# A decoder step with paged attention and experts: the key steps of the samples moved into the projections, three of four of their products on GpSimd

## What is computed

```python
h = rmsnorm(x);  p = h @ w_in                       # 1024 -> 2560 columns
q, k, v, u = rope(rmsnorm(q)), rope(rmsnorm(k)), v, ua * sigmoid(ub)
# differential attention, 4 heads, 2 components of 64 each, v of 128
a = softmax(q1 k1) - lam * softmax(q2 k2);  o = rmsnorm(a @ v) * (1 - lam_init)
# prompt: causal over 512 tokens.  sample b: over 4096 cached tokens, 32 pages
# of 128 given by page_table, and its own new one
conv = silu(layernorm(causal_depthwise_conv31(u)))
x = x + concat(o, conv) @ w_out
x = x + moe(rmsnorm(x))                             # 32 experts, the best 4 of each token
```

## Time and profile before

| | us |
|---|---|
| median of 3 runs | 1733.65 |
| lowest and highest | 1730.45, 1736.07 |
| the profiled execution | 1735.41 |
| its span in the trace | 1733.7 |
| PE busy | 1474.0 (85%) |
| DVE busy | 782.4 (45%) |
| ACT busy | 356.0 (21%) |
| POOL busy | 96.7 (6%) |

### The profile page before, as it was taken

How to read it: one execution, slowest core, us unless ns; L and a number is a source line. 1 busy time by engine, 2 the same in 40 slices (tenths; PEclk the granted TensorE clock), 3 DMA queues, 4 the chain that set the end, 5 groups by cost and what they waited for, 6 DMA issues and landing times.

```text
span 1733.7 us, 32093 instructions
## 1 busy us (share of the span) xinstructions
PE 1474.0 (85%) x11950; PEld 595.0 (34%) x11951; DVE 782.4 (45%) x1160; ACT 356.0 (21%) x822; POOL 96.7 (6%) x173
## 2 busy tenths in 40 slices
PE   3868887779788978899998998999899999899970
PEld 2433333346433354332332332333233332232320
DVE  2789879997786335221332232132132131131326
ACT  3212212222222111111211211212112122121220
POOL 0000010000000000000100000000000000000000
PEclk8989995679898857999999999999899999999995
DMA  9557888988998785598999999999999999999986
GB/s 327 182 187 258 283 295 272 331 279 292 311 301 270 242 352 207 227 392 339 429 420 403 427 417 396 412 418 411 392 421 412 401 428 411 397 428 399 428 351 253
DMA packets 127292, 598.10 MB, mean 345 GB/s; under 512 B 20503, under 2 KB 20517, under 8 KB 102026
## 3 DMA queue, kind: packets, MB, share of 16 engines
q1 hardware_dynamic: 109088, 560.20, 81.9%
q10 hardware_dynamic: 8634, 20.00, 3.4%
q0 software_dynamic: 9504, 17.06, 2.6%
HBM read 589.36 MB, written 25.87 MB: 355 GB/s over the span
## 4 chain that ended last, share of the span: by engine, by line
PE 40%; DMA 19%; DVE 2%; issue 1%; ACT 0%; DVEq 0%; SPq 0%; ACTq 0%
PE bank L1511 25%; DMA wts<-in_w_gate_up 16%; PE bank L1548 8%; PE bank L1530 4%; DMA wts<-in_w_down 3%; PE bank L1501 1%; PE bank L1618 1%; DVE v_ring L2139 1%; PE bank L1559 1%; PE bank L1599 0%; DVE q_b L2139 0%; DMA h_tok<-h_rows,v_tok 0%; ACT k_T L1155 0%; DVEq L2127 0%; ACT k_T L1138 0%
## 5 line engine op out<-in xcount | busy, mean ns | idle before, releaser
L1511 PE MATMUL bank<-wts,h_T 128*32 128x512 f32 x4032 | 443.9, 597 | 9.7 <-DMA wts<-in_w_gate_up 5.2
L2061 DVE TENSOR_SCALAR q_T<-bank 128x512 f32<-128x512 f32 x32 | 22.1, 692 | 636.9 <-PE bank L1511 636.9
L1511 PEld LDWEIGHTS bank<-wts,h_T 128*32 128x32 f32 x4032 | 129.5, 111 | 308.3 <-issue 296.4
L1548 PE MATMUL bank<-wts,k_T 128*32 128x512 f32 x2048 | 228.3, 597 | 8.0 <-issue 4.9
L1530 PE MATMUL bank<-wts,h_T 128*32 128x512 f32 x992 | 132.6, 675 | 52.2 <-DMA wts<-in_w_gate_up 50.4
L1658 DVE TENSOR_TENSOR wts<-wts,q_b 128x1024 f32<-128x1024 f32 x128 | 158.1, 1235 | 23.1 <-DMA wts<-in_cache_k 17.4
L1661 DVE TENSOR_REDUCE sc<-wts 128x16 f32<-128x1024 f32 x128 | 156.2, 1220 | 4.4
L1145 ACT ACTIVATE h_T<-bank 128x512 f32<-128x512 f32 x66 | 35.9, 595 | 573.5 <-PE bank L1501 573.5
L1548 PEld LDWEIGHTS bank<-wts,k_T 128*32 128x32 f32 x2048 | 64.9, 110 | 149.0 <-issue 139.5
L1223 PE MATMUL bank<-wts,h_T 128*8 128x128 f32 (+1 forms) x480 | 92.7, 465 | 12.3 <-ACT h_T L854 6.4
L1155 ACT ACTIVATE k_T<-bank 32x256 f32<-32x256 f32 x256 | 95.7, 374 | 13.6 <-PE bank L1548 10.2
(11 more groups left out here) (330 smaller groups left out, 1375.8 us busy)
## 6 DMA issues: line engine op xcount, KB each, us to landing
wts<-in_w_gate_up SPq DMA_DIRECT2D x126, 2048.0 KB, 15.8
wts<-in_w_down SPq DMA_DIRECT2D x64, 2048.0 KB, 18.3
wts<-in_cache_k SPq DMA_DIRECT2D x256, 256.0 KB, 3.7
v_ring<-in_cache_v SPq DMA_DIRECT2D x160, 256.0 KB, 3.8
wts<-in_cache_v SPq DMA_DIRECT2D x96, 256.0 KB, 3.9
wts<-in_w_in SPq DMA_DIRECT2D x5, 2048.0 KB, 24.1
wts<-y_rows SPq DMA_DIRECT2D x4, 2048.0 KB, 15.1
wts<-in_w_out ACTq DMA_DIRECT2D x8, 512.0 KB, 6.2
```

The source lines that it names most:

```text
L1511: m = nc.tensor.matmul(PS[part][p0:p0 + 32, :], lhs[:, 32 * b:32 * b + 32], rhs[:, part * F + half * 512:part * F + half * 512 + 512], sta ...
L1548: m = nc.tensor.matmul(PS[4][p0:p0 + 32, :], act_T[0][:, k, a0:a0 + 32], chunk[c][:, k, n * 512:(n + 1) * 512], start=(c == 0 and k == 0), ...
```

## The change

The weights of the schedule change, and 60 of the first 80 key products go to GpSimd. In the projections a key weight of 1 becomes 1.45 (`KEYS`), the value weights stay. In the units the key weights are 0.2 and 0, the value weights 1, 0.9 and 1. In the convolution a stage has 2.5 key and 1.6 value steps in place of 2 and 2, an L stage 1.2 and 1 in place of 1 and 1. For a key step with a number below 80 that is not 3 modulo 4, GpSimd makes the product, as two pieces of 128x512 in place, one for each page, and VectorE waits for them (`kprod_done`) and only sums. For this GpSimd walks the list too; its `tap_w` products and index constants become stages of Q and L. Two sets of semaphores, `xw_loaded` and `y_loaded`, are merged into one, `rows_in`. The core of the diff:

```diff
+        KEYS = 1.45
         for s in range(1, TILES + 1):
             if s > 1:
-                plan(("P", s), 1, both=s > 2)
-            plan(("P", s - 1), 1 if s > 1 else 0, both=s > 2)
-            plan(("P", s), 1 if s > 1 else 3, both=s > 2)
+                plan(("P", s), KEYS, values=1 if s > 2 else 0)
+            plan(("P", s - 1), KEYS if s > 1 else 0, values=1 if s > 2 else 0)
+            plan(("P", s), KEYS if s > 1 else 3, values=1 if s > 2 else 0)
...
-            plan(("P", s), 1)
-            plan(("P", s), 1, 1, 1, both=True)
+            plan(("P", s), KEYS)
+            plan(("P", s), *[KEYS] * 3, values=1)
             if s < TILES:
-                plan(("P", s + 1), 1, both=True)
-            plan(("P", s), 2, values=1)
-            plan(("P", s), 1, 1, both=True)
+                plan(("P", s + 1), KEYS, values=1)
+            plan(("P", s), 2 * KEYS, values=1)
+            plan(("P", s), *[KEYS] * 2, values=1)
...
             if j < UNITS:
-                plan(("Q", j), 1, both=True)
+                plan(("Q", j), 0.2, values=1)
...
             if j < UNITS:
-                plan(("Q", j), 0.4, values=0.7)
+                plan(("Q", j), 0, values=0.9)
...
             if j > 1 and (j - 1) % H == 0:
-                plan(("N", (j - 1) // H), 1, both=True)
-        plan(("V", 0), *[2] * (CT + 1), both=True)
+                plan(("N", (j - 1) // H), 0, values=1)
+        plan(("V", 0), *[2.5] * (CT + 1), values=1.6)
         for n in range(CT + 1):
-            plan(("V", 1), 2, both=True)
-            plan(("L", 0), 1, both=True)
+            plan(("V", 1), 2.5, values=1.6)
+            plan(("L", 0), 1.2, values=1)
...
+        PIECE = 512
+        KEYS_ON_POOL, KEYS_SHARED = (3, 4), 80
+        def on_pool(n):
+            return n < KEYS_SHARED and n % KEYS_ON_POOL[1] < KEYS_ON_POOL[0]
+        def products_on_pool(n):
+            return sum(on_pool(m) for m in range(n + 1)) * GP * (AW // PIECE)
...
+            def key_step(b, g):
+                r, n = g % RING, b * NG + g
+                if not on_pool(n):
+                    return
+                if first_on_pool(b) == g:
+                    pool.wait_ge(qb_in, 32 if b == 0 else 16 * (b + 1))
+                pool.wait_ge(k_full[r], 16 * GP * (4 * b + g // RING + 1))
+                for p in range(GP):
+                    for c0 in range(0, AW, PIECE):
+                        cols = slice(c0, c0 + PIECE)
+                        nc.gpsimd.tensor_tensor(k_ring[:, r, p, cols], k_ring[:, r, p, cols],
+                                                q_b[:, b % 2, cols], ALU.mult).then_inc(kprod_done, 1)
...
-                dve.wait_ge(k_full[r], 16 * GP * (4 * b + g // RING + 1))
-                V.link(mul(k_ring[:, r, :, :], k_ring[:, r, :, :],
-                           q_b[:, b % 2, :].unsqueeze(1).to_broadcast([P, GP, AW])))
+                if on_pool(b * NG + g):
+                    dve.wait_ge(kprod_done, products_on_pool(b * NG + g))
+                else:
+                    dve.wait_ge(k_full[r], 16 * GP * (4 * b + g // RING + 1))
+                    V.link(mul(k_ring[:, r, :, :], k_ring[:, r, :, :],
+                               q_b[:, b % 2, :].unsqueeze(1).to_broadcast([P, GP, AW])))
                 total(sc[:, b % LEAD, GP * g:GP * (g + 1), :],
                       k_ring[:, r, :, :].rearrange("p g (h d) -> p g h d", d=QD)).then_inc(kred_done, 1)
```

More of the change, by code:

```diff
@@ L239, in hybrid_step @@
                 continue
[L240 to L241 removed]
+            plan(("P", s), KEYS)
+            plan(("P", s), *[KEYS] * 3, values=1)
             if s < TILES:
[L243 to L245 removed]
+                plan(("P", s + 1), KEYS, values=1)
+            plan(("P", s), 2 * KEYS, values=1)
+            plan(("P", s), *[KEYS] * 2, values=1)
             if s < TILES:
[L247 to L248 removed]
+                plan(("P", s + 1), KEYS, values=1)
+        plan(("P", TILES), *[KEYS] * 2, values=1)
         plan(("Q", 0), 0)
@@ L341, in hybrid_step @@
         v_full = [sem(f"v_full{n}") for n in range(VRING)]
-        xw_loaded = [sem(f"xw_loaded{n}") for n in range(TILES + 1)]
+        rows_in = [sem(f"rows_in{n}") for n in range(TILES + 1)]
         win_in = [sem(f"win_in{n}") for n in range(5)]
@@ L345, in hybrid_step @@
         w_used = [sem(f"w_used{n}") for n in range(6)]
-        y_loaded = [sem(f"y_loaded{n}") for n in range(TILES + 1)]
         last_full = [sem(f"last_full{n}") for n in range(2)]
@@ L720, in _, with value_step @@
+            def value_step(b, g):
+                pass
+            run_with_samples(key_step, value_step, {part: part_q(part[1]) if part[0] == "Q" else
+                                                    part_l(part[1]) if part[0] == "L" else iter(())
+                                                    for part in a_no})
             bound, rows_0 = pool.alloc_register("bound"), pool.alloc_register("rows_0")
```

89 lines of the change are left out of this document (49 added, 40 removed).

## The result

The changed kernel took 1770.76 us (median of 4 runs, 1766.15 to 1774.36); the kernel before, in 4 runs beside it, 1733.35. The ratio is 1.0215, interval 1.0185 to 1.0244: 2.1% slower, 47 us above the range's upper end. The profiled execution took 1774.36 us (span 1772.7), 39 us more than the one of before.

The account below looks back on a forecast made before the run. VectorE, busy with key steps, was taken to bound most of the front, whose shift moves the end equally. Projections -10, units -27, convolution +7 and router -5 summed to -35 us: 1699 us, range 1664 to 1724.

Parts of the forecast that it names:

- the projections' 201 us: Projections: the stage would take 201 us in place of 211, 10 saved.
- four limits of 161 to 205 us coupled by four slots: Projections: limits from VectorE (191), shared access (164), transfers (187 to 205) and SyncE's issues (161), coupled by the key ring.
- VectorE's own limit: Projections: VectorE alone would give 191 us, 175 of work and idle time plus 16 for exclusion by GpSimd.
- the lock: Projections: GpSimd and VectorE's two-input operations exclude one another, reductions are free of it; 16 us, bounds 0 and 31.
- Units: Attention units: 23 key steps leave, TensorE becomes the bound; 88 us in place of 115, 27 saved.
- rival B: Whole front: VectorE's saving comes through nearly whole, TensorE's clock rises in the units; -70 us, 1664 us; chance 0.2.
- Convolution: Convolution stretch: six more key steps on VectorE, partly hidden; 7 us longer, bounds 0 and 14.
- Router: Output product and router: four key steps fewer on VectorE; 5 us saved, bounds 0 and 9.6.
- GpSimd's piece: GpSimd's 128x512 product: 0.95 us each, 115 us for the 60 key products.
- C: Projections: loads become the bound, the stage keeps its 211 us or gains some; end near 1715 us; chance 0.2.
- D: Front: offloading does not help, exclusion and pieces of 1.45 us take back the saving; 1735 us; chance 0.05.
- E: Projections: GpSimd's piece costs by instruction, 1.91 us, the stage gets 67 us longer; 1776 us; chance 0.07.

Follow-up runs that it names:

- e5: Changed kernel without 124 of its 128 key loads and the waits for them: 1719.6 us, projections 217.6 us.
- e11: Changed schedule with all key products on VectorE and 124 of 128 key loads left out: 1744.3 us, projections 243.1 us.
- e4: Changed kernel with SyncE issuing each value load two value steps later: 1752.6 us, ratio 1.0112 to the kernel before.
- e13: Changed kernel with key loads of only 128 of a page's 512 columns after the ring's first round: 1758.8 us.
- e16: Changed kernel with both value loads two value steps later and key loads of 128 of 512 columns after the first round: 1737.4 us.
- e10: Changed schedule with all key products on VectorE and value loads two value steps later: 1755.0 us, ratio 1.0119.
- e1: Changed schedule with all 128 key products on VectorE, none on GpSimd: 1765.8 us, ratio 1.0198.
- e17: Kernel before, its schedule kept, with every second key product from the hundredth on at GpSimd: 1734.5 us, ratio 1.0008.
- e7: Changed kernel with GpSimd's products cut into pieces of 256 columns: 1772.3 us.
- e15: Changed kernel with one GpSimd instruction of 128x1024 per key step in place of two pieces: 1774.0 us, ratio 1.0242.
- e2: Schedule of the kernel before, with the first 80 key products shared with GpSimd as in the change: 1740.0 us, ratio 1.0042.

## Why the prediction was wrong

**The step that failed is the projections' 201 us**, "four limits of 161 to 205 us coupled by four slots", of which I took one near the largest: 10 saved where 56 to 58 were lost. Two terms of it failed.

The first is VectorE's own limit. It was put at 191 us, 172 of work and 19 of waits. e5, with no load to wait for, has VectorE 192.5 us busy and 25 idle (17.5 of it for ScalarE, 5.4 for GpSimd), 217.6 together: 27 above the limit, and above the 213.3 of before. Some 15 of the 27 are the lock, put at 16 us, and 6 the waits. Against e11, which has the same schedule and loads and no key product on GpSimd, the same instructions of VectorE are longer by 31 us in e5, the 22 key products alone by 12.5:

```profile
L1706 DVE TENSOR_TENSOR wts<-wts,q_b 128x1024 f32<-128x1024 f32 x22 | 40.0, 1818 | 0.2
```

In the changed kernel, where GpSimd stands still more, the lock is 21 us: the key products are longer by 22 x (1.455 - 1.256) = 4.4, the rotary operations by 9.2 (their means 1.161, 1.822, 1.699 and 1.483 us for 0.687, 1.218, 1.226 and 1.217), the eight small products on `cw` by 3.0 (0.655 for 0.286) and a dozen other small instructions by 4; the sum had counted neither of the last two.

The second and larger is the 51 us of the loads, from 217.6 to 269. The sum took a maximum where the costs are stages of one round. A slot is loaded, multiplied by GpSimd, summed by VectorE and only then loaded again, through a queue that also waits for value products, which wait for VectorE. e4, e13 and e16 show that two of these delays, the place of the value loads and the length of a key load, add up (20.6, 16.6, together 33.9 us); that the other 17 are the round through four slots fits, but is argued. The sum had seen the danger, "only 50 us are left for waits" on SyncE, and priced it at nothing over the largest limit; the queue waited 86 us.

**Without the offload the simple sum holds.** 82 steps x 2.39 + 35 + 19 = 250 us for a moved schedule with all products on VectorE: e10 took 249.8, e11 243.1, and e1, where value loads stand ahead of key loads as in the changed kernel, 261.2. A moved key step costs its 2.39 us in the projections and gives back 1 in the units. Only the offload could have turned that round, and even without loads it gave back 25 of the 37 us that the move cost.

**Units: right in the number, in part by luck.** -26 us by the cut of the earlier trace rows, -22 by first and last event, -27 forecast; e1, e5 and e10 show the same 93 to 95 whatever happens ahead of them. But the 88 us were TensorE's busy time at the old clock. The clock rose to 0.79 from 0.68, TensorE is busy 71 us of the 89 (87 of 115 before), and the stage did not follow it down. What stands in its place are waits of a unit's own chain, which the forecast had set aside: TensorE waits 13 us for exponents of ScalarE, about as before (14), and VectorE, now idle a third of the stage, 20. VectorE's wait, from the first maxima to the first convolution product:

```profile
DVE stq L1812 <- ACT qk L1014: 19.6, 14, 3.0
```

A higher clock alone did not bring rival B's 70 us.

**Convolution: right**, +2 to +4 of the forecast +7. **Router: wrong**, -5 forecast, +6 by the cut and +2 by events; VectorE's busy time fell by 6 us and the time did not, so VectorE is not the bound that the forecast had taken it for from 61 busy of 70 us. e17 says less about it: it took 14 products, 17 us, off VectorE there and in the convolution's second half, but only 5 us of its busy time went, since other instructions took longer, and the time stayed. What the bound is there was not looked for. **Expert loop: right**, 1074 us.

**GpSimd's piece: mis-sized**, 0.95 us against 1.26 undisturbed and 1.41 in the mean; 120 pieces made 165 us busy for 115. The estimate of 1.12 us worked out from the Trainium skill's "GPSIMD Engine Reference", section "Elementwise — side-by-side cycle accounting", is the nearer, and 11% too low; the trace decides. By e7 and e15 GpSimd's work, 19 us more or less, moved the end by nothing that can be told.

**The rivals.** C named the mechanism, loads as the bound of the projections, and stopped at "keeps its 211 us": right in kind, wrong by 58 us in size, since it counted the queue's issue time and not the waits that stand in order in it. D's warning, the one of the Trainium skill's "Perfetto Trace Analysis", section "Optimizing Scalar/DVE Operations", came true in its verdict (the offload gains nothing: e1 against the changed kernel, e2 against before). The lock is a good part of why, but not all: without loads 59 products, some 74 us, leave VectorE from e11 to e5, 31 come back as longer instructions, the reductions keep their 1.22 us beside GpSimd, and the stage is 25 us shorter. It is the loads that take these 25 away. E's 1776 is near the 1771 measured by accident: it asked for a piece of over 1.56 us.

## What to carry to other kernels

Where work is handed from one engine to another through a ring with few slots, add up the round (issue, landing, first engine, second engine, the queue's other entries) and divide it by the slots; a maximum over the engines' busy times can be the time only if the ring is deep enough to hide the rest. Here issue 1.32, landing 3.6, two pieces 2.5 and a reduction 1.2 us are 8.6, over four slots 2.2 us a step as an estimate; a step took 3.3 (269 / 82). So the round alone is a lower bound, and the waits of the queue in its order come on top. Before moving work into a stage, leave out its loads in one run: the gap to the full version says what the feeding costs, and here it was 51 us after the change against 7 before it (18 with the move alone). An in-order queue shared by two rings is best asked which entry waits with a ready one behind it; moving that entry later gave back 20 us in one line, though in the kernel before, where the queue had little to catch up, nothing that can be told. And what is taken off an engine must be set against what the taker holds up: by the trace of e5, 31 of 74 us.

## What the runs showed of the hardware that was not expected

GpSimd's in-place product of two full float32 inputs takes 0.18 us and 1.08 us for each 512 columns, and the products of the convolution weights, whose inputs repeat, 1.91 us for 1024 columns. Beside it small operations of VectorE take longer as well, and not only those with two inputs of many columns: its 128x128 products on `cw` took 0.655 us in the mean, for 0.286 before, and its operations on 128x2 elements in the units of e2 0.548 for 0.170, while reductions of 128x1024 kept 1.22. With a quarter of the bytes of a page the landing went not to a quarter, but from 3.6 to 1.9 us. And TensorE's granted clock in the projections fell from 0.91 to 0.82 with the waits: 544 products took 186.6 us where 532 took 172.0, and e5, in which TensorE idles 42 us and not 82, is at 0.91 with 176.0 for 543. So the waits cost TensorE time beyond their own length.
